# Two attention layers as a two-step pipeline: scores one step ahead, transposes in PSUM banks of their own

## What is computed

```python
def masked_softmax(s, mask):
    s = jnp.where(mask, s, NEG_INF)
    m = jnp.max(s, axis=-1, keepdims=True)
    p = jnp.where(mask, jnp.exp(s - m), 0.0)
    return p, jnp.sum(p, axis=-1, keepdims=True), m
...
s = q @ k.T * dh ** -0.5 + position_bias      # masked
p, den, m = masked_softmax(s, mask)
out = (p / den) @ v
```

## Time and profile before

| | us |
|---|---|
| median of 3 runs (1890.61 to 1898.06) | 1893.71 |
| profiled execution, its own time | 1888.3 |
| its span, first to last instruction | 1886.5 |
| PE busy | 1794.1 (95%) |
| DVE busy | 1222.6 (65%) |
| ACT busy | 935.6 (50%) |
| compressed layer's loop, first scores to the output product | 1104.25 to 1249.82 |
| dilated layer's loop, the same | 1516.11 to 1666.05 |

### The profile page before, as it was taken

How to read it: one execution, slowest core, us unless ns; L and a number is a source line. 1 busy time by engine, 2 the same in 40 slices (tenths; PEclk the granted TensorE clock), 3 DMA queues, 4 the chain that set the end, 5 groups by cost and what they waited for, 6 DMA issues and landing times.

```text
span 1886.5 us, 31683 instructions
## 1 busy us (share of the span) xinstructions
PE 1794.1 (95%) x13416; PEld 1684.9 (89%) x13416; DVE 1222.6 (65%) x1918; ACT 935.6 (50%) x1280; POOL 124.1 (7%) x35
## 2 busy tenths in 40 slices
PE   7999999999999999999999978799999988889998
PEld 6999999999889999999998877569998977779996
DVE  6976766877569767668775657556554734456453
ACT  5446565544355465655443546445443654445442
POOL 2612000000017120000000000000000000000000
PEclk9899999999999999999999999789999998899999
DMA  8684445555546644455555462224555645225552
GB/s 235 163 235 147 149 157 186 167 183 179 202 140 188 192 144 148 157 191 166 180 179 205 135 181 91 90 67 157 179 201 194 182 139 134 90 90 184 185 211 79
DMA packets 249148, 305.75 MB, mean 162 GB/s; under 512 B 9778, under 2 KB 224142, under 8 KB 249007
## 3 DMA queue, kind: packets, MB, share of 16 engines
q1 hardware_dynamic: 235959, 289.66, 47.7%
q10 hardware_dynamic: 13048, 14.07, 3.5%
HBM read 299.51 MB, written 4.19 MB: 161 GB/s over the span
## 4 chain that ended last, share of the span: by engine, by line
PE 76%; DVE 10%; DMA 6%; ACT 5%; issue 2%; DVEq 1%; ACTq 0%; SPq 0%
PE psum L463 23%; PE psum L464 23%; PE psum L465 23%; DVE wlo L439 3%; DMA raw<-in_b_w_q 2%; ACT whi L431 2%; DMA raw<-in_w_ffn_gate 2%; PE psum L2385 1%; DMA raw<-in_a_w_in 1%; DMA raw<-in_b_w_out 1%; ACT work L2018 1%; DVE work L2246 1%; DMA x<-in_x 1%; DMA raw<-in_a_w_out 1%; DVE hT L617 0%
## 5 line engine op out<-in xcount | busy, mean ns | idle before, releaser
L431 ACT ACTIVATE whi<-raw 128x2048 fp32r<-128x2048 f32 (+2 forms) x277 | 526.6, 1903 | 552.3 <-PE psum L465 177.6
L439 DVE TENSOR_TENSOR wlo<-raw,whi 128x2048 fp32r<-128x2048 f32 x249 | 563.3, 2281 | 183.3 <-PE psum L465 158.7
L463 PE MATMUL psum<-hT,whi 128*128 128x256 f32 x2160 | 616.9, 286 | 7.5 <-DVE wlo L439 3.8
L464 PE MATMUL psum<-hT,whi 128*128 128x256 f32 x2160 | 613.0, 284 | 0.0
L465 PE MATMUL psum<-hT,wlo 128*128 128x256 f32 x2160 | 612.9, 284 | 0.0
L463 PEld LDWEIGHTS psum<-hT,whi 128*128 128x128 f32 x2160 | 416.4, 193 | 10.9 <-issue 5.5
L464 PEld LDWEIGHTS psum<-hT,whi 128*128 128x128 f32 x2160 | 416.5, 193 | 0.1
L465 PEld LDWEIGHTS psum<-hT,wlo 128*128 128x128 f32 x2160 | 416.2, 193 | 0.0
L439 POOL TENSOR_TENSOR wlo<-raw,whi 128x2048 fp32r<-128x2048 f32 (+1 forms) x28 | 122.8, 4390 | 585.6 <-ACT whi L431 402.7
L463 PE MATMUL psum<-whi,hT 128*128 128x256 f32 (+2 forms) x448 | 145.1, 324 | 1.1 <-issue 1.1
L465 PE MATMUL psum<-whi,hT 128*128 128x256 f32 (+2 forms) x448 | 144.3, 322 | 0.0
(11 more groups left out here) (352 smaller groups left out, 2832.0 us busy)
## 6 DMA issues: line engine op xcount, KB each, us to landing
raw<-in_w_in SPq DMA_DIRECT2D x78, 1024.0 KB, 5.7
raw<-in_ffn_w_up SPq DMA_DIRECT2D x44, 1024.0 KB, 5.2
raw<-in_w_ffn_gate SPq DMA_DIRECT2D x22, 1024.0 KB, 5.4
raw<-in_w_ffn_up SPq DMA_DIRECT2D x22, 1024.0 KB, 6.4
raw<-in_w_ffn_down SPq DMA_DIRECT2D x22, 1024.0 KB, 5.0
raw<-in_ffn_w_down SPq DMA_DIRECT2D x22, 1024.0 KB, 5.2
raw<-in_b_w_q SPq DMA_DIRECT2D x12, 1024.0 KB, 5.7
raw<-in_a_w_in SPq DMA_DIRECT2D x10, 1024.0 KB, 5.8
```

Source lines behind the costliest of these rows:

```text
L431: act.activation(part(whi, n, HIGH_SLOTS), part(raw, n, RAW_SLOTS), ACT.Copy).then_inc(high_made, 1)
L439: eng.tensor_tensor(part(wlo, n, LOW_SLOTS), part(raw, n, RAW_SLOTS), part(whi, n, HIGH_SLOTS).bitcast(F32), ALU.subtract).then_inc(stream ...
L463: nc.tensor.matmul(dst, left[0], right[0], start=first, stop=False)
L464: nc.tensor.matmul(dst, left[0], right[1], start=False, stop=False)
```

## The change

In both loops the scores run one step ahead, and the transposes get banks that the scores don't use. Every step's weights, maxima and sums now have two buffers (even and odd steps). On PE, `scores(s + 1)` is issued in step s and waits for M(s) instead of `copies(s)`. On DVE, M(s + 1) stands before W(s). On ACT, `copies(s - 1)` stands after `exps(s)`.

In the dilated layer the transposes of a step are cut in chunks of up to four blocks: three in an even step, two in an odd one. The chunks alternate between banks 5 and 7, so each waits until ACT has copied the chunk two before it. The halves of the units a, b, c are placed by a table `FILL`. All fills past the first nine share bank 4. The context is collected in one bank and taken to SBUF by DVE (`take_context`).

```diff
+            def turns(s):
+                _, t, _, _ = step(s)
+                if t:
+                    return (((0, 0), (0, 1), (0, 2), (0, 3)), ((0, 4), (0, 5), (1, 0), (1, 1)),
+                            ((1, 2), (1, 3), (1, 4), (1, 5)))
+                return ((0, 0), (0, 1), (0, 2)), ((1, 0), (1, 1), (1, 2))
+            def turn_bank(m):
+                return bank((5, 7)[m % 2])
+            for g in range(QUADS - 1):
+                a, b, c = ([(LEAD + ND * g + i, j) for j in range(2)] for i in range(ND))
+                FILL[4 * g - 1], FILL[4 * g] = (None, None, a[0]), (a[1], None, b[0])
+                FILL[4 * g + 1], FILL[4 * g + 2] = (b[1], None, c[0]), (None, c[1], None)
...
                 def scores(s):
                     if s:
-                        pe.wait_ge(turned_copied.sem, turned_copied.at(2 * s))
+                        pe.wait_ge(maxima_ready.sem, maxima_ready.at(2 * s))
                 def turn(s):
+                    for m, blocks in enumerate(turns(s), turns_until(s)):
+                        if m >= 2:
+                            pe.wait_ge(turned_copied.sem, turned_copied.at(m - 1))
+                        pe.wait_ge(probs_ready.sem, probs_ready.at(2 * s + blocks[-1][0] + 1))
...
                 for s in range(STEPS):
-                    scores(s)
+                    fill(s, 0)
+                    if s + 1 < STEPS:
+                        scores(s + 1)
+                    fill(s, 1)
                     if s:
                         context(s - 1)
                     turn(s)
+                    fill(s, 2)
...
                     exps(s)
-                    if u < count and i >= 2:
-                        evict(u + i - 1)
-                    if s and s % 2 == 0:
-                        high(s // 2 - 1)
-                    copies(s)
-                    if u < count and i == 0:
-                        evict(u)
+                    if u < count and i == 3:
+                        evict(u + 2)
+                    if s:
+                        copies(s - 1)
+                    if u < count and i < 2:
+                        evict(u + i)
+                    if s >= 4 and s % 2 == 0:
+                        high(s // 2 - 2)
...
+                maxima(0)
                 for s in range(STEPS):
+                    if s + 1 < STEPS:
+                        maxima(s + 1)
+                    weigh(s)
+                    if s and s % 2 == 0:
+                        take_context(s // 2 - 1)
                     if s % 4 < 3:
                         make_lows(dve, n0 + min(LEAD + ND * (s // 4) + s % 4 + 2, count + 2))
```

More of the change, by code:

```diff
@@ L1770, in compressed_attention_layer, with columns, most, den @@
             TURN_HIDDEN, KEY_OUT, VALUE_OUT, CMP_SCORES, CMP_TURN = (13, 14), 15, 16, (17, 18), (19, 20)
[L1771 to L1776, removed]
+            GROUP_BLOCKS = (21, 22)
+            products = 23
+            FILL = {0: ((6, 0), (6, 1)), 1: ((7, 0), (7, 1)), 2: ((8, 0), (8, 1)), 3: ((9, 0), None), 4: ((9, 1), None),
+                    5: ((10, 0), None), 6: ((11, 0), None), 7: ((12, 0), None), 8: ((13, 0), None), 9: ((14, 0), (14, 1))}
+            def columns(first, s):
+                first += 12 * (s % 2)
+                return stat[:, first:first + 4].rearrange("p (e a) -> p e a", e=2)
+            def most(s):
+                return columns(60, s)
+            def den(s):
+                return columns(64, s)
+            def rec(s):
+                return columns(68, s)
+            def probs_s(s):
+                return odd_probs[s >= 8] if s % 2 else even_probs
             def step(s):
@@ L1939, in context @@
                     g = j // 2
[L1940 removed]
+                    if g >= 2 and s % 4 == 0:
+                        pe.wait_ge(group_taken.sem, group_taken.at(g - 1))
+                    b = bank(4 + g % 2)[:, (j % 2) * S + t * P:(j % 2) * S + (t + 1) * P]
+                    last = g < 2 and s % 4 == 3
                     for n in range(2 * (t + 1)):
@@ L2228, in _, with maxima @@
                 dve.wait_ge(table_load.sem, table_load.at(16 * (P // ROWS + 2)))
-                for s in range(STEPS):
+                def maxima(s):
                     j, t, keys = step(s)
@@ L2391, in turn @@
                 def turn(s):
[L2392 to L2396, removed]
+                    for m, blocks in enumerate(turns(s), turns_until(s)):
+                        if m >= 2:
+                            pe.wait_ge(turned_copied.sem, turned_copied.at(m - 1))
+                        pe.wait_ge(probs_ready.sem, probs_ready.at(2 * s + blocks[-1][0] + 1))
+                        for i, (e, n) in enumerate(blocks):
+                            mm = nc.tensor.transpose(turn_bank(m)[:, i * P:(i + 1) * P],
+                                                     probs[:, 2 * (s % 2) + e, n * P:(n + 1) * P], ident)
                         mm.then_inc(probs_turned.sem, 1)
@@ L2414, in context, with fill @@
                         mm.then_inc(context_ready.sem, 1)
-                for i in range(2 * LEAD):
-                    dense_half(i)
-                i = 2 * LEAD
+                def fill(s, which):
+                    if s in FILL and FILL[s][which]:
+                        dense_half(*FILL[s][which])
+                for n in range(LEAD):
+                    for j in range(2):
+                        dense_half(n, j)
+                scores(0)
+                fill(-1, 2)
                 for s in range(STEPS):
-                    scores(s)
-                    if i < 2 * count:
-                        dense_half(i)
-                        i += 1
+                    fill(s, 0)
+                    if s + 1 < STEPS:
+                        scores(s + 1)
+                    fill(s, 1)
                     if s:
@@ L2426, in _ @@
                     turn(s)
-                    if s % 2 == 0 and i < 2 * count:
-                        dense_half(i)
-                        i += 1
+                    fill(s, 2)
                 context(STEPS - 1)
```

244 lines of the change are left out of this document (155 added, 89 removed).

## The result

The changed kernel takes 1949.3 us (median of 4 runs, 1942.18 to 1954.89); the kernel before, beside it, 1892.2 (4 runs, 1887.38 to 1898.06). The ratio is 1.0298, 95% interval 1.0253 to 1.0344: slower, by 57 us. The forecast was 1944 within 1908 to 1962.

The account below looks back on a forecast made before the run. The prediction took chains of dependent steps, with a 9.2 us low part-DMA-high part trip, to bound the loops, no engine being full. Compressed -10 and dilated +61 gave +51 on 1893.7: 1944 us, range 1908 to 1962.

Parts of the forecast that it names:

- the sum: Both loops together: -10 us for the compressed loop and +61 for the dilated loop, +51 in all.
- the compressed loop's term: Compressed loop: scores running a step ahead shorten it to 135 us, -10 us, with no ACT wait for DMA.
- The step that decided, the dilated loop: Dilated loop: PE's last transposes wait for weights, low part, DMA, high part, exps and copy; +51 us, +61 with the clock.
- the walk: Dilated loop, one quad between ends of W: 22.2, 12.0, 16.2 and 10.0 us, 60.4 in all; loop 201 at full clock.
- term for the clock: Dilated loop: six idle spells, each followed by half-clock work losing 1.6 to 2.2 us, +10 us added once.
- round trips: Dilated loop: low part to DMA to high part, 9.2 us each, three in series per quad, nine trips.
- the prediction's six: Dilated loop: two idle spells of 9 to 11 us per quad, six counted for the clock; counting nine would give +17.
- Sum 66.5: Compressed loop: M and W 46 us, PE work between them 66.5, start 7, end 8.7; 128, plus 7 for low clock.
- The text's own bound, 143: Compressed loop: if it stays above 143 us, the estimated heads and tails of PE's work are too short.
- Round trips half hidden: Rival, dilated loop: only the stall at step 4g's third chunk bites; loop 167 us, +17, total 1904; chance 0.08.
- Faster: Rival: the pipeline works if no highs hold ACT; dilated loop 136 us, -14, total 1870; chance 0.09.

Follow-up runs that it names:

- compressed_only: The kernel before with only the compressed layer's loop changed: 1884.54 us, ratio 0.9973 to the kernel before.
- both_old_first: The changed kernel with dilated low parts a step earlier, high parts behind the copies, and the compressed layer of before: 1873.58 us, ratio 0.9909.
- lows_early: The changed kernel with each low part in the dilated loop made one step earlier, so its DMA issues earlier: 1871.32 us, ratio 0.9916.
- high_behind: The changed kernel with each dilated-loop high part moved on ACT behind the next copies, transfers as late: 1888.21 us, ratio 0.9996.

## Why the prediction was right

In the profiled executions the changed kernel's span is 60.7 us longer, where the sum had 51. Of the 9.7 us between, 2.9 are the compressed loop's term, 1.9 the dilated loop's, and 4.7 lie ahead of the first loop, where nothing was changed; over the twelve profiled executions that loop started between 1101.3 and 1109.5 us. Both loops' terms were too favourable, so neither made up for the other.

**The step that decided, the dilated loop, held in place, cause and size.** W(s) ends on DVE at 1524.66 (s = 0), 1548.08, 1560.10, 1578.17 and 1587.70 (s = 4). The legs from one to the next are 23.4, 12.0, 18.1 and 9.5 us, where the walk (the prediction's sum from one end of W to the next) had 22.2, 12.0, 16.2 and 10.0; the second quad's are 24.7, 11.9, 17.8 and 9.5. Rows of the changed kernel's timeline from which two of them come (last W of steps 1 and 2):

```profile
1547.66 0.42 DVE L2650 TENSOR_SCALAR work<-work,stat 128x384 f32<-128x384 f32 x1
...
1559.48 0.62 DVE L2650 TENSOR_SCALAR work<-work,stat 128x768 f32<-128x768 f32 x1
```

The walk held no term for the clock; that was added once for the loop. The two legs that hold a long wait of PE are those that came out longer, by 1.2 to 2.5 us, about the 1.6 to 2.2 that each wait was to cost. That the excess is the clock's is argued from the size and the place; no run varied the clock alone. The quads were to take 55.8, 60.4, 60.4 and 24.4 at full clock and took 58.6, 64.1, 64.1 and 26.1: 212.9 in place of 201 + 10. From the low part's start to ACT's next own work eight of the nine round trips took 9.0 to 9.3 us; one took 10.6 (low part 1674.91, high part from 1683.70 on), because its transfer took 6.5 us and not 5.

**Six stretches at the low clock on the chain, and three beside it.** Windows of the changed kernel right after three of the six long waits and, in the second group, after the three short waits of PE ahead of `context(4g + 1)` (1.43, 1.15 and 1.53 us):

```profile
1535.60:1540.00 4.40, 4.40 (x22) 4.40 (x23) 0.00 (x0) 0.98 (x2) 0.00 (x0) 0.53 0.00 0
...
1599.30:1603.00 3.70, 3.70 (x18) 3.70 (x19) 0.00 (x0) 1.02 (x2) 0.00 (x0) 0.50 0.02 4
...
1663.00:1667.00 4.00, 3.98 (x22) 3.98 (x23) 0.00 (x0) 1.04 (x2) 0.00 (x0) 0.62 0.00 0
```

```profile
1560.10:1564.00 3.90, 1.85 (x20) 1.44 (x20) 2.62 (x2) 1.57 (x5) 0.00 (x0) 1.00 0.00 0
1624.30:1628.00 3.70, 1.86 (x20) 1.45 (x20) 2.82 (x4) 1.90 (x6) 0.00 (x0) 1.00 0.00 0
1688.30:1692.00 3.70, 1.86 (x20) 1.45 (x20) 2.83 (x4) 1.89 (x6) 0.00 (x0) 1.00 0.00 0
```

After all six long waits PE ran at 0.50 to 0.62, its 1.2 GHz level for most of the window; after the short ones at 1.00, the 2.4 GHz level. So the prediction's six was the better count for the chain. The Trainium skill ("TensorE: Matmul & The Clock Gate", section on HAM oscillation) describes turns whose wait for a DMA is longer than their matmuls; that the short waits count too was the prediction's reading, and the page does not say it. The windows agree with the page on the six long waits.

The clock nevertheless fell nine times in this loop. The other three falls are at the fill of steps 1, 5 and 9, which neither count had. In steps 1 and 9:

```profile
1550.34:1554.00 3.66, 3.66 (x19) 3.66 (x20) 0.00 (x0) 0.00 (x0) 0.00 (x0) 0.58 0.67 218
1677.25:1682.00 4.75, 4.75 (x22) 4.75 (x23) 0.00 (x0) 0.00 (x0) 0.00 (x0) 0.50 0.64 217
```

Ahead of each PE had stood idle for 1.1 us, transposed for 1.0 and stood idle for 1.6 more, waiting for a low part. These stretches lengthen PE's busy time and not the chain: the maxima behind that fill were ready at 1556.8 in step 1, and the next W waited for exps until 1558.4. The legs that hold them took 12.0 us in the first quad and 11.9 in the second, as in the walk (13.3 in the third, with the longer round trip).

**The compressed loop's term was mis-sized, with its sign right.** The step "Sum 66.5 ... together 128, and 7 for stretches at the low clock: 135, compressed loop -10" gave in the changed kernel 138.5, -7.1, and that was among its best. Over the twelve profiled executions the loop took 144.2, 145.6, 148.5 and 148.5 us in the old order (mean 146.7) and 138.5, 138.6, 141.6, 143.2, 143.4, 144.1, 144.2 and 145.5 in the new (mean 142.4): -4.3, and `compressed_only` gained 0.27%, 5 us. The text's own bound, 143, was passed in five of eight. Nor was ACT free of waits for a DMA there, as the text expected: the changed kernel has one, of 2.8 us. Windows of that whole loop, in `compressed_only` and in `both_old_first` (first row new order, second old):

```profile
1107.70:1249.32 141.62, 111.93 (x884) 94.42 (x885) 94.27 (x346) 77.56 (x196) 0.00 (x0) 0.84 0.25 83
```

```profile
1103.80:1252.32 148.52, 118.81 (x885) 98.26 (x885) 94.10 (x343) 77.35 (x194) 0.00 (x0) 0.80 0.24 80
```

PE's idle time is the same in both, 29.7 us; over the twelve executions it is 29.0 to 31.7 us in the old order and 29.6 to 30.9 in the new. What differs is how long the same matmuls take, 115.2 to 118.8 us in the old order and 107.6 to 115.9 in the new, with mean clocks of 0.80 to 0.83 and 0.83 to 0.88. So the pipeline did not shorten PE's idle time; what it gained is matmuls done at the higher clock. Two parts of the reason are in the changed kernel's trace. At the end, W(15) is done at 1236.9 and the output product starts at 1247.44:

```profile
1237.38 0.60 ACT L2103 ACTIVATE work<-psum 128x512 f32<-128x512 f32 x1 [2.64 <-PE psum L1921]
...
1239.01 1.98 PE L1971 MATMUL psum<-work 128*64 128x128 f32 x16 [1.66 <-ACT work L2058]
...
1243.94 0.69 DVE L2299 TENSOR_TENSOR work<-psum,work 128x512 f32<-128x512 f32 x1 [7.05 <-PE psum L1930]
```

These are 10.5 us, where the prediction had 8.7 and before had 4.8: `context(14)` waits for copies that stand behind the new copy of the blocks (L2103). And inside the loop, in the waits of the same kernel, DVE still stands idle ahead of the maxima, and PE ahead of the transposes:

```profile
DVE work L2276 <- PE psum L1944: 30.6, 13, 6.7
...
PE psum L1956 <- DVE work L2292: 24.7, 26, 3.5
```

In all eight executions of the new order PE's 6.6 us of waits for copies ahead of the scores are gone. In their place stand 3.0 us ahead of one fill (for nothing that the profile shows), 1.7 to 2.9 ahead of the contexts for copies, and 22.3 to 24.7 us for W ahead of the transposes, where the old order had 20.6 to 24.6. Why the stretches at the low clock fall where they do in one execution and not in another was not settled.

**The rivals.** "Round trips half hidden" needed two of the three transfers of a quad to land behind fills; all nine were waited for, 6.6 us or more. "Faster" named its condition, no high part holding ACT, and its price for the loop, 136 us: `lows_early`, which meets the condition, has 136.7. Its 1871.3 us lie near the rival's 1870 by luck: the kernel before took 1887.7 beside it and not the 1893.7 from which the rival counted, so it gained 16 us and not 24, and its compressed loop took 143.2 us and not 135. The rival was a good account of the dilated loop of another kernel.

## What to carry to other kernels

When work is moved behind something else in an engine's queue, look for what in front of it waits for a DMA, and whether that DMA is released by the step in progress: with the same late round trip of 9.2 us PE was idle for 26 to 30 us of the loop where little stood behind it in ACT's queue (the kernel before, and `high_behind`), and for 84 where the copies did. The fix was not in the pipeline: freeing the slot one step earlier turned +3.0% into -0.8%, and with the high part behind the copies as well it is -1.2% (the last two intervals overlap). Try the order of the queue and the release of the buffer apart, then together; and time one layer by itself, since a loop's own variation with the clock (here 7 us for one order) hides a gain of 5 in a single profile.

## What the runs showed of the hardware

The rise of the clock is seen in the starts of like matmuls. Changed kernel, PE, fill behind the wait that ended at 1599.30:

```profile
1604.26 0.41 PE L468 MATMUL psum<-query_rows,whi 128*128 128x256 f32 x1
1604.47 0.35 PE L469 MATMUL psum<-query_rows,wlo 128*128 128x256 f32 x1
...
1604.78 0.28 PE L468 MATMUL psum<-query_rows,whi 128*128 128x256 f32 x1
```

The starts are 0.21 us apart until 1604.47 and 0.12 after it: about half the rate for the first 5.2 us of work, then all of it. That length is this wait's own: behind the one that ended at 1663.02 the granted clock was 0.50 for 3.0 us and 0.97 in the microsecond after. The same compressed loop, with no line changed, came out between 144.2 and 148.5 us (old order) and between 138.5 and 145.5 (new) in different executions, with mean granted clocks from 0.80 to 0.88. From the issue on SyncE to ACT's start the transfer of one raw slot (1 MB) took 4.9 to 5.2 us in eight of the nine round trips of the changed kernel's dilated loop, for example 5.04 (1526.88 to 1531.92) and 5.09 (1590.26 to 1595.35), and 6.5 in one (1677.22 to 1683.70), for a reason that was not found. Before the change one took 5.10 (1567.85 to 1572.95), in a quad with half as much again of traffic (117 GB/s in the earlier trace rows, 75 here). No run varied the other traffic alone.
